# Scan of two directions: one group of transposes moved from round 5 of a step to round 3

## The chip, the cores and the metric

The kernel is one program on one core of a Trainium2 chip. The metric is the device time of one execution in microseconds (us). TensorE, VectorE, ScalarE and GpSimd each run their own queue in program order; semaphores order the queues against each other. SyncE issues the transfers.

## The reference, cut to what matters

Two blocks follow each other. The first has two layers; in each the tokens (16 meta tokens and 1024 others, L = 1040) pass through a latent attention and a bidirectional recurrence side by side, then through a mixture of experts. The recurrence has 8 heads with a 64 x 64 state each and runs once forward and once backward:

```python
def step(S, inp):
    r_t, w_t, k_t, v_t, kk_t, b_t = inp
    sa = jnp.einsum('bhvk,bhk->bhv', S, kk_t)
    S = S * w_t[:, :, None, :] - sa[..., None] * b_t[:, :, None, :] + v_t[..., None] * k_t[:, :, None, :]
    return S, jnp.einsum('bhvk,bhk->bhv', S, r_t)
```

Here b_t = kk * a. Two key forms enter the state: k (with its gate), "index 0", and -kk * a, "index 1". The change touches the second.

## The kernel before, in words

**The scan in chunks.** The scan doesn't go token by token. A step takes C = 104 tokens (two chunks of H = 52) of one direction; NT = 10 steps make one direction of a layer, so there are 2 layers x 2 directions x 10 = 40 steps. The tile `hb` holds the two key forms scaled by a running decay: index 0 from k (VectorE, L1570) and index 1 from kk * a (GpSimd L1638, then VectorE L1561). The tile `kr` holds the scaled kk and r (L1565, L1568). The products of hb and kr give the small matrices `Ab` (from index 1) and `Ak` (from index 0), which VectorE takes out of PSUM with a mask (L1576). From Ab comes a matrix `lm` (GpSimd masks, L1653), and from it T in five levels of products, `ps<-T,lm`, `ps<-XX,T`, `ps<-T,XX`. At the end of the step the state is advanced with the turned, that is transposed, hb: tile `m.tm`, named hbT in the profile, read only there.

**Rounds.** Each step is a list of phases in 23 rounds (`PHASES`): rounds 0 to 2 hold phases 0 to 10, round 3 phase 11, round 4 phase 12, round 5 phases 13 and 14, round 6 phase 15, rounds 7 to 22 phases 16 to 31. The backward direction runs 11 rounds (`STAGGER`) behind the forward one. In a round each engine does the phases of one direction, then a piece of an attention item (`att_pe`, `att_dve`), then the phases of the other direction; ScalarE does its longest attention piece, the exponentials, at the round's end. A direction in its rounds 0 to 3 comes second, else the forward one comes first. When one direction is in rounds 3 to 6, the other is in its last levels and then in its state products (`ps<-S,kr` and others).

**What the phases around the change do.**
- Phase 3: TensorE turns v (use 2); ScalarE copies it in phase 5.
- Phases 8 to 11: VectorE makes hb index 1, kr, and hb index 0. GpSimd makes rka in phase 11 (L1644).
- Phase 12: the first products, kr with hb index 1; phase 13: the second products, kr with hb index 0.
- Phase 14: TensorE turns hb index 0, then index 1, then multiplies for the bonus (`ps<-aa,rk`). ScalarE copies the three results. GpSimd makes lm with index 0.
- Phase 15: TensorE turns lm (`ps<-consts,lm`), VectorE adds the identity (L1581, L1585, L1588).

**Banks and uses.** A direction has two PSUM banks in the scan. The results of a step are numbered as uses; use n stands in bank n % 2, and before it is written `scan_free` waits until use n - 2 has been taken out, by ScalarE if its number is in `BY_ACT`, else by VectorE. Uses in the kernel before: 2 turned v; 3, 4 first products; 5, 6 second products; 7 turned hb index 0; 8 turned hb index 1; 9 bonus; 10 turned lm. A turn is written as a product with the identity, so in the trace turned hb is `ps<-consts,hb`, and each turn or product of the scan leaves two matmul records.

Of the kernel before, what the change touches and what calls it, by code (L numbers as in the profile page):

```python
# [1180 lines left out]
USES = 34  # L1181
LEVELS = 6
MASKS = {14: 0, 15: 1, 16: 2, 18: 3, 20: 4, 22: 5}
BY_ACT = {2, 7, 8, 9} | {13 + 3 * lv for lv in range(4)} | {25 + 4 * x + n for x in range(2) for n in (0, 1, 3)}
ODD = [(slice(64 * o, 64 * o + 64), slice(64 * o, 64 * o + H)) for o in range(2)]


# [63 lines left out]
def scan_bank(P, d, step, use):  # L1251
    return P.ps[2 * d + use % 2]
# [102 lines left out]
def scan_pe(e, P, li, d, step, ph):  # L1355
# [11 lines left out]
    if ph == 3:  # L1367
        scan_free(e, P, li, d, step, 2)
        b = scan_bank(P, d, step, 2)
        turns(e, P, [(b[r, 256 * ch + 64 * j:256 * ch + 64 * j + 64], rw.v[q, j, half(d, step, ch)])  # L1370
                   for ch in range(2) for j in range(4) for q, r in ODD]).then_inc(*pe.tick(*key, 2))
    if 12 <= ph < 14:
        e.wait_ge(*dv.at(*key, "kr1" if ph == 12 else "hb0"))
        mat = 1 if ph == 12 else 0
        for ch in range(2):
            use = 2 * ph - 21 + ch
            b, hs = scan_bank(P, d, step, use), slice(H * ch, H * ch + H)
            scan_free(e, P, li, d, step, use)
            at = [2 * H * (place(1, ch, j) // 4 * 2 + j // 2) for j in range(4)]
            mms(e, [(b[r, at[j]:at[j] + 2 * H].rearrange("p (a t) -> p a t", a=2),  # L1380
                     m.hb[q, mat, j, hs], m.kr[q, j, :, hs], True, True) for j in range(4) for q, r in ODD]
                ).then_inc(*pe.tick(*key, use))
    if ph == 14:
        for k in range(2):
            b = scan_bank(P, d, step, 7 + k)
            scan_free(e, P, li, d, step, 7 + k)
            turns(e, P, [(b[r, 256 * ch + 64 * j:256 * ch + 64 * j + 64], m.hb[q, k, j, H * ch:H * ch + H])
                       for ch in range(2) for j in range(4) for q, r in ODD]).then_inc(*pe.tick(*key, 7 + k))
        scan_free(e, P, li, d, step, 9)
        e.wait_ge(*po.at(*key, "rka"))  # L1390
        mms(e, [(scan_bank(P, d, step, 9)[32 * d:32 * d + 8, 0:C], rw.rk8[:, j, :], m.aa[:, j, :], j == 0, j == 3)
                for j in range(4)]).then_inc(*pe.tick(*key, 9))
# [43 lines left out]
    if ph >= 26:  # L1436
        x, part = divmod(ph - 26, 3)
        ch, S, use = m.chunks[x], m.S[x], 25 + 4 * x
        if part == 0:
            if x == 0:  # L1440
                e.wait_ge(*dv.at(*key, "T", 5))
                e.wait_ge(*ac.at(*key, "T", 5))
                e.wait_ge(*ac.at(*key, "ev", 2))
                e.wait_ge(*dv.at(*key, "ev", 6))
            else:
                e.wait_ge(*ac.at(*key, "ev", use - 1))
            e.wait_ge(*(dv.at(*key, "fS", x) if step or x else dv.at(li, d, "S0")))
            mms(e, state_rows(P, d, m, S, ch, m.vt[:, ch, :])).then_inc(*pe.tick(*key, use))
        if part == 1:
            e.wait_ge(*ac.at(*key, "ev", use))  # L1450
            mms(e, [(P.ps[2 * d + j % 2][r, 64 * (j // 2):64 * (j // 2) + 64], m.TT[c, 4 * ch + j, :],
                     m.rh[c, split_columns(j)], True, True) for j, o, r, c in quarters(range(4))]
                ).then_inc(*pe.tick(*key, use + 1))
        if part == 2:
            b = scan_bank(P, d, step, use + 2)
            mats = []
            for j in range(4):
                jc = slice(64 * j, 64 * j + 64)
                mats += [(b[q, jc], m.tm[r, 0, ch, jc], m.vt[r, ch, jc], True, False) for q, r in ODD]
                mats += [(b[q, jc], m.tm[r, 1, ch, jc], m.uu[r, split_columns(j)], False, True) for q, r in ODD]  # L1460
            e.wait_ge(*ac.at(*key, "ev", use + 1))
            mms(e, mats).then_inc(*pe.tick(*key, use + 2))
            mms(e, outputs(scan_bank(P, d, step, use + 3), m, S, ch, m.vt[:, ch, :])).then_inc(*pe.tick(*key, use + 3))


def scan_act(e, P, li, d, step, ph):
    rw, pe, dv, ac, po = P.rw, P.c("scan_pe"), P.c("scan_dve"), P.c("scan_act"), P.c("scan_pool")
    m, sl, key = P.scan[d], chunk(d, step), (li, d, step)

    def take(out, view, use):  # L1470
        e.wait_ge(*pe.at(*key, use))
        e.activation(out, view, ACT.Copy).then_inc(*ac.tick(*key, "ev", use))

    if ph == 1:
        e.wait_ge(*dv.at(*key, "ev", 0))
        e.activation(m.sig, m.sig, ACT.Tanh, scale=0.5).then_inc(*ac.tick(*key, "sig"))
        e.wait_ge(*dv.at(*key, "ev", 1))
        e.activation(m.aa, m.aa, ACT.Tanh, scale=0.5).then_inc(*ac.tick(*key, "aa"))
    if ph == 5:
        take(m.vt[0:HP].rearrange("p c n -> p (c n)"), scan_bank(P, d, step, 2)[0:HP, :], 2)  # L1480
    if ph == 5:
        e.wait_ge(*po.at(*key, "b"))
        for j in range(4):
            made = e.activation(m.aa[:, j, :], m.aa[:, j, :], ACT.Identity, bias=rw.par[:, 7, j:j + 1],
                                scale=rw.par[:, 1, j:j + 1])
        made.then_inc(*ac.tick(*key, "1+"))
    if ph == 6:
        e.wait_ge(*dv.at(*key, "x1"))
        e.activation(m.ei, m.cs if d == 0 else m.x1, ACT.Exp, scale=KAPPA).then_inc(*ac.tick(*key, "ei"))
    if ph == 7:  # L1490
        e.activation(m.eK, m.x1 if d == 0 else m.cs, ACT.Exp, scale=-KAPPA if d == 0 else KAPPA).then_inc(
            *ac.tick(*key, "eK"))
    if ph == 8:
        e.activation(m.ea, m.cs if d == 0 else m.x1, ACT.Exp, scale=-KAPPA).then_inc(*ac.tick(*key, "ea"))
    if ph == 9:
        e.wait_ge(*dv.at(*key, "f"))
        e.activation(m.f, m.f, ACT.Exp, scale=-0.5 * KAPPA).then_inc(*ac.tick(*key, "f"))
    if ph == 14:
        for k in range(2):
            take(m.tm[0:HP, k, :, :].rearrange("p c n -> p (c n)"), scan_bank(P, d, step, 7 + k)[0:HP, :], 7 + k)  # L1500
        take(rw.bon[d][:, sl], scan_bank(P, d, step, 9)[32 * d:32 * d + 8, 0:C], 9)
    if 16 <= ph < 26 and level_of(ph)[1]:
        lv = level_of(ph)[0]
        out, bank = joined(m.T)[0:HP, 1], joined_bank(P.ps[2 * d + 1])[0:HP]
        if lv < 5:
            take(out, bank, 10 + 3 * lv)
        else:
            e.wait_ge(*pe.at(*key, 24))
            e.activation(out[:, 1], bank[:, 1], ACT.Copy).then_inc(*ac.tick(*key, "T", 5))
    if ph >= 26:  # L1510
        x, part = divmod(ph - 26, 3)
        use = 25 + 4 * x
        if part == 0:
            take(halves(m.rh)[0:HP], P.banks[0:HP, 2 * d:2 * d + 2, 0:128], use)
        if part == 1:
            take(halves(m.uu)[0:HP], P.banks[0:HP, 2 * d:2 * d + 2, 0:128], use + 1)
        if part == 2:
            if step and x == 0:
                e.wait_ge(*P.d(f"scan_y{d}_out").at(li, step - 1, 3))
            take(m.ys[0:HP, m.chunks[x], :], scan_bank(P, d, step, use + 3)[0:HP, 0:256], use + 3)  # L1520


def scan_dve(e, P, li, d, step, ph):
# [47 lines left out]
    if 12 <= ph < 14:  # L1571
        dst = m.ab if ph == 12 else m.ak
        for ch in range(2):
            use = 2 * ph - 21 + ch
            e.wait_ge(*pe.at(*key, use))
            e.tensor_tensor(dst.rearrange("p (k c i) a t -> p k c i (a t)", k=2, c=2)[0:HP, :, ch],  # L1576
                            scan_bank(P, d, step, use)[0:HP, 0:416].rearrange("p (k i x) -> p k i x", k=2, i=2),
                            m.qmask, ALU.mult).then_inc(*dv.tick(*key, "ev", use))
# [51 lines left out]
def scan_pool(e, P, li, d, step, ph):  # L1630
# [14 lines left out]
    if ph in MASKS:  # L1645
        lv = MASKS[ph]
        if lv == 0:
            e.wait_ge(*dv.at(*key, "ev", 4))
        elif lv == 2:
            e.wait_ge(*dv.at(*key, "T", 0))  # L1650
        elif lv > 2:
            e.wait_ge(*pe.at(*key, 8 + 3 * (lv - 2)))
        e.tensor_tensor(m.LM[lv % 2][0:HP], m.ab[0:HP, :, 0, :],  # L1653
                        bc(m.lmask[0:HP, H * lv:H * lv + H].unsqueeze(1), [HP, 8, H]), ALU.mult).then_inc(
            *po.tick(*key, "lm", lv))
# [2721 lines left out]
```

## Time and profile before

| | |
|---|---|
| median of 3 runs | 5022.56 us (5014.44 to 5028.41) |
| profiled execution | 5016.12 us, its span 5014.2 us |
| mean granted TensorE clock | 0.955 |
| busy, share of the span | TensorE 90%, weight loads 76%, VectorE 64%, ScalarE 43%, GpSimd 24% |
| scan of layer 0 | 367 to 1135 us |
| scan of layer 1 | 2249 to 3020 us |

The busy shares are means over stages with different limits. In the scan the rounds of the two directions and the attention items are woven together, so the rows in order of time are the ones to read: "idle before" in brackets says how long the engine stood idle before the instruction and what ended it. Instructions of one kind that follow each other are merged into one row.

### The profile page before, as it was taken

To read this page: it belongs to the slowest core of one execution; us is meant where nothing else is said; L and a number is where in the kernel's file an instruction comes from. 1 tells how busy PE (TensorE), PEld (TensorE's weight loads), DVE (VectorE), ACT (ScalarE), POOL (GpSimd) and SP (SyncE) were. 2 spreads that over 40 slices of the span, in tenths; PEclk is the share of its full clock that TensorE was granted. 3 is DMA by queue.
4 is the path that set the end of the run, shared out by engine and by line. 5 is a ranking of instruction groups with operands and counts; after the bars stand their busy time and mean duration, and the time that the engine had idled before them with its cause. 6 is when DMAs were issued, how large, how long until landed. Compare 5 with 4: busy or idle time off the path is not lost. (4 is left out here: it accounts for less than half of the span.)

```text
span 5014.2 us, 126170 instructions
## 1 busy us (share of the span) xinstructions
PE 4497.6 (90%) x55574; PEld 3831.9 (76%) x55574; DVE 3209.2 (64%) x4913; ACT 2168.0 (43%) x3971; POOL 1220.1 (24%) x868
## 2 busy tenths in 40 slices
PE   6988888889799978988888889799979988999999
PEld 6887777776588857878778777688857647788887
DVE  5436666668788875346666569688874476561752
ACT  2433333333288863333333333388853252332431
POOL 0012222222244420002222222244421100222221
PEclk9999999999899988999999999899989889999999
DMA  5420111013366665420101013466751002333333
GB/s 145 149 59 19 36 22 33 21 42 112 120 241 251 256 200 136 126 57 21 35 20 34 20 47 126 171 243 259 263 202 46 22 1 101 106 93 126 111 107 97
DMA packets 379005, 535.80 MB, mean 107 GB/s; under 512 B 118165, under 2 KB 302549, under 8 KB 350413
## 3 DMA queue, kind: packets, MB, share of 16 engines
q1 hardware_dynamic: 335645, 488.54, 30.2%
q0 software_dynamic: 41472, 33.95, 2.2%
q8 instruction: 441, 7.23, 0.6%
q10 hardware_dynamic: 1344, 5.24, 0.3%
q14 instruction: 103, 0.84, 0.1%
HBM read 573.10 MB, written 121.92 MB: 139 GB/s over the span
## 5 line engine op out<-in xcount | busy, mean ns | idle before, releaser
L288 PE MATMUL ps<-w_hi,xbT 128*128 128x512 f32 x1536 | 502.9, 399 | 19.1 <-DVE w L2833 19.1
L288 PE MATMUL ps<-hT,w_in 128*128 128x416 f32 (+1 forms) x2736 | 491.5, 338 | 4.1 <-DVE hT L3113 4.1
L288 PEld LDWEIGHTS ps<-hT,w_in 128*128 128x128 f32 x2736 | 455.7, 194 | 29.6 <-issue 19.2
L2833 DVE TENSOR_TENSOR w<-w,w_hi 128x2048 fp32r<-128x2048 f32 x192 | 430.1, 2279 | 2.2 <-ACT w_hi L2790 2.2
L1653 POOL TENSOR_TENSOR lm<-Ab,consts 116x416 f32<-116x416 f32 x240 | 268.5, 1130 | 514.1 <-DVE T L1588 252.5
L2790 ACT ACTIVATE w_hi<-w 128x2048 fp32r<-128x2048 f32 x192 | 359.1, 1937 | 0.0
L288 PEld LDWEIGHTS ps<-w_hi,xbT 128*128 128x128 f32 x1536 | 290.9, 189 | 87.2 <-DVE w L2833 28.3
L288 PE MATMUL ps<-w,xbT 128*128 128x512 f32 x768 | 301.7, 393 | 0.0
L2864 DVE TENSOR_TENSOR w<-w,w_hi 128x2048 fp32r<-128x2048 f32 x96 | 223.3, 2326 | 97.2 <-ACT w_hi L2826 97.2
L288 PE MATMUL ps<-w_hi,actT 128*128 128x512 f32 x768 | 253.6, 391 | 4.9 <-DVE actT L2859 4.9
L288 PE MATMUL ps<-x1T,w_gate 128*128 128x512 f32 x1056 | 248.4, 391 | 3.0 <-DVE x1T L3800 1.6
L288 PE MATMUL ps<-x1T,w_up 128*128 128x512 f32 x1056 | 246.5, 389 | 0.0
L288 PE MATMUL ps<-w_down,act 128*128 128x512 f32 x1056 | 241.3, 391 | 3.1 <-POOL w_down L4026 3.1
L288 PEld LDWEIGHTS ps<-x1T,w_gate 128*128 128x128 f32 x1056 | 199.3, 189 | 45.2 <-issue 1.9
L288 PEld LDWEIGHTS ps<-w_down,act 128*128 128x128 f32 x1056 | 199.2, 189 | 44.8 <-POOL w_down L4026 3.5
L1596 DVE TENSOR_TENSOR XX<-ps,consts 116x416 f32<-116x416 f32 x200 | 117.7, 588 | 175.2 <-PE ps L288 174.7
L288 PEld LDWEIGHTS ps<-x1T,w_up 128*128 128x128 f32 x1056 | 198.3, 188 | 41.1
L4017 POOL TENSOR_TENSOR w_up<-w_up,w_up 128x1024 fp32r<-128x1024 f32 x44 | 116.4, 2646 | 458.1 <-ACT w_up L3939 458.1
L288 PE MATMUL ps<-w_out,mixT 128*104 128x512 f32 (+1 forms) x864 | 218.2, 406 | 10.5 <-DVE w_out L2171 5.8
L2779 POOL DMA_INDIRECT t_ys<-yo,slots x96 | 101.5, 1057 | 463.4 <-PE ps L295 384.7
L288 PEld LDWEIGHTS ps<-w_out,mixT 128*104 128x104 f32 (+1 forms) x864 | 151.7, 179 | 67.7 <-DVE w_out L2171 10.2
L794 POOL TENSOR_TENSOR w_in<-w_in,w_in 128x1024 fp32r<-128x1024 f32 x22 | 56.1, 2549 | 605.2 <-ACT w_in L809 605.2
(464 smaller groups left out, 11015.9 us busy)
## 6 DMA issues: line engine op xcount, KB each, us to landing
w<-in_moe_w_dram SPq DMA_DIRECT2D x192, 1024.0 KB, 12.5
w_gate<-in_w_gate_dram SPq DMA_DIRECT2D x44, 512.0 KB, 3.8
w_up<-in_w_up_dram SPq DMA_DIRECT2D x44, 512.0 KB, 3.9
w_down<-in_w_down_dram SPq DMA_DIRECT2D x44, 512.0 KB, 3.6
w_in<-in_w_in_dram SPq DMA_DIRECT2D x36, 512.0 KB, 4.9
w_out<-in_w_out_dram SPq DMA_DIRECT2D x24, 512.0 KB, 6.9
t_h<-x SPq DMA_DIRECT2D x20, 416.0 KB
kn<-t_kn SPq DMA_DIRECT2D x8, 1040.0 KB, 7.3
```

The source lines that it names most:

```text
L288: made = e.matmul(out, a, b, start=start, stop=stop)
L794: e.tensor_tensor(w.lo, w.x, w.hf, ALU.subtract).then_inc(*count.tick(li, "lo", n))
L1596: e.tensor_tensor(m.XX[0:HP].rearrange("p (k u) t -> p k u t", k=2), both_banks(P, d, 0)[0:HP].rearrange("p k (u t) -> p k u t", t=H), bc( ...
L1653: e.tensor_tensor(m.LM[lv % 2][0:HP], m.ab[0:HP, :, 0, :], bc(m.lmask[0:HP, H * lv:H * lv + H].unsqueeze(1), [HP, 8, H]), ALU.mult).then_i ...
L2779: e.indirect_dma_start(T["ys"], bass.IndirectOffsetOnAxis(P.slots[:, table_column(b - 2):table_column(b - 2) + 1], 0), m.yo[b % 2], None, ...
L2790: e.activation(w.hi, w.x, ACT.Copy).then_inc(*P.c("moe_act").tick(li, "w13", b, k))
L2833: e.tensor_tensor(w.lo, w.x, w.hf, ALU.subtract).then_inc(*P.c("moe_dve").tick(li, "w13", b, k))
L2864: e.tensor_tensor(w.lo, w.x, w.hf, ALU.subtract).then_inc(*dv.tick(li, "w2", b))
L4017: e.tensor_tensor(w.lo, w.x, w.hf, ALU.subtract).then_inc(*po.tick(0, c, "lo", f))
```

## The change

TensorE turns hb index 1 in phase 11 (round 3) and not in phase 14 (round 5); ScalarE's copy of it moves to phase 11 too. The turn is now use 3 and the uses after it are renumbered: 4, 5 first products; 6, 7 second products; 8 turned hb index 0; 9 and 10 as before. So the second of the first products (use 5) waits for ScalarE's copy of use 3, where it waited for ScalarE's copy of turned v; the turn of index 0 (use 8) waits for the first Ak to be taken, as before; the bonus (use 9) waits for the second Ak to be taken, where it waited for ScalarE's copy of turned hb. `BY_ACT` and the waits on "ev" numbers follow. No instruction that computes is added or taken away.

```diff
--- before.py
+++ after.py
@@ -1181,7 +1181,7 @@
 USES = 34
 LEVELS = 6
 MASKS = {14: 0, 15: 1, 16: 2, 18: 3, 20: 4, 22: 5}
-BY_ACT = {2, 7, 8, 9} | {13 + 3 * lv for lv in range(4)} | {25 + 4 * x + n for x in range(2) for n in (0, 1, 3)}
+BY_ACT = {2, 3, 8, 9} | {13 + 3 * lv for lv in range(4)} | {25 + 4 * x + n for x in range(2) for n in (0, 1, 3)}
 ODD = [(slice(64 * o, 64 * o + 64), slice(64 * o, 64 * o + H)) for o in range(2)]
 
 
@@ -1369,11 +1369,18 @@
         b = scan_bank(P, d, step, 2)
         turns(e, P, [(b[r, 256 * ch + 64 * j:256 * ch + 64 * j + 64], rw.v[q, j, half(d, step, ch)])
                    for ch in range(2) for j in range(4) for q, r in ODD]).then_inc(*pe.tick(*key, 2))
+    if ph in (11, 14):
+        k, use = (1, 3) if ph == 11 else (0, 8)
+        b = scan_bank(P, d, step, use)
+        scan_free(e, P, li, d, step, use)
+        e.wait_ge(*dv.at(*key, f"hb{k}"))
+        turns(e, P, [(b[r, 256 * ch + 64 * j:256 * ch + 64 * j + 64], m.hb[q, k, j, H * ch:H * ch + H])
+                   for ch in range(2) for j in range(4) for q, r in ODD]).then_inc(*pe.tick(*key, use))
     if 12 <= ph < 14:
         e.wait_ge(*dv.at(*key, "kr1" if ph == 12 else "hb0"))
         mat = 1 if ph == 12 else 0
         for ch in range(2):
-            use = 2 * ph - 21 + ch
+            use = 2 * ph - 20 + ch
             b, hs = scan_bank(P, d, step, use), slice(H * ch, H * ch + H)
             scan_free(e, P, li, d, step, use)
             at = [2 * H * (place(1, ch, j) // 4 * 2 + j // 2) for j in range(4)]
@@ -1381,11 +1388,6 @@
                      m.hb[q, mat, j, hs], m.kr[q, j, :, hs], True, True) for j in range(4) for q, r in ODD]
                 ).then_inc(*pe.tick(*key, use))
     if ph == 14:
-        for k in range(2):
-            b = scan_bank(P, d, step, 7 + k)
-            scan_free(e, P, li, d, step, 7 + k)
-            turns(e, P, [(b[r, 256 * ch + 64 * j:256 * ch + 64 * j + 64], m.hb[q, k, j, H * ch:H * ch + H])
-                       for ch in range(2) for j in range(4) for q, r in ODD]).then_inc(*pe.tick(*key, 7 + k))
         scan_free(e, P, li, d, step, 9)
         e.wait_ge(*po.at(*key, "rka"))
         mms(e, [(scan_bank(P, d, step, 9)[32 * d:32 * d + 8, 0:C], rw.rk8[:, j, :], m.aa[:, j, :], j == 0, j == 3)
@@ -1441,7 +1443,7 @@
                 e.wait_ge(*dv.at(*key, "T", 5))
                 e.wait_ge(*ac.at(*key, "T", 5))
                 e.wait_ge(*ac.at(*key, "ev", 2))
-                e.wait_ge(*dv.at(*key, "ev", 6))
+                e.wait_ge(*dv.at(*key, "ev", 7))
             else:
                 e.wait_ge(*ac.at(*key, "ev", use - 1))
             e.wait_ge(*(dv.at(*key, "fS", x) if step or x else dv.at(li, d, "S0")))
@@ -1495,9 +1497,10 @@
     if ph == 9:
         e.wait_ge(*dv.at(*key, "f"))
         e.activation(m.f, m.f, ACT.Exp, scale=-0.5 * KAPPA).then_inc(*ac.tick(*key, "f"))
+    if ph == 11:
+        take(m.tm[0:HP, 1, :, :].rearrange("p c n -> p (c n)"), scan_bank(P, d, step, 3)[0:HP, :], 3)
     if ph == 14:
-        for k in range(2):
-            take(m.tm[0:HP, k, :, :].rearrange("p c n -> p (c n)"), scan_bank(P, d, step, 7 + k)[0:HP, :], 7 + k)
+        take(m.tm[0:HP, 0, :, :].rearrange("p c n -> p (c n)"), scan_bank(P, d, step, 8)[0:HP, :], 8)
         take(rw.bon[d][:, sl], scan_bank(P, d, step, 9)[32 * d:32 * d + 8, 0:C], 9)
     if 16 <= ph < 26 and level_of(ph)[1]:
         lv = level_of(ph)[0]
@@ -1571,7 +1574,7 @@
     if 12 <= ph < 14:
         dst = m.ab if ph == 12 else m.ak
         for ch in range(2):
-            use = 2 * ph - 21 + ch
+            use = 2 * ph - 20 + ch
             e.wait_ge(*pe.at(*key, use))
             e.tensor_tensor(dst.rearrange("p (k c i) a t -> p k c i (a t)", k=2, c=2)[0:HP, :, ch],
                             scan_bank(P, d, step, use)[0:HP, 0:416].rearrange("p (k i x) -> p k i x", k=2, i=2),
@@ -1645,7 +1648,7 @@
     if ph in MASKS:
         lv = MASKS[ph]
         if lv == 0:
-            e.wait_ge(*dv.at(*key, "ev", 4))
+            e.wait_ge(*dv.at(*key, "ev", 5))
         elif lv == 2:
             e.wait_ge(*dv.at(*key, "T", 0))
         elif lv > 2:
```

## Rows read from the trace of the kernel before

**Rows 1.** Page, the chain that ended last, by engine, as share of the span.
```profile
PE 15%; DVE 1%; DMA 0%; issue 0%; SPq 0%; ACT 0%; POOL 0%; POOLq 0%; DVEq 0%
```

**Rows 2.** Stretches, both scans: from:to, length, busy us by engine, clock, DMA.
```profile
367.00:1135.00 768.00, 676.12 (x19597) 607.64 (x19597) 501.34 (x1090) 294.46 (x829) 211.27 (x197) 0.98 0.13 30
2249.00:3020.00 771.00, 670.51 (x19528) 610.75 (x19528) 472.99 (x1029) 278.85 (x765) 208.42 (x197) 0.95 0.14 35
```

**Rows 3.** Tile hb: its instructions, then what their engines waited for.
```profile
L288 PE MATMUL ps<-consts,hb x2560: 215/216/258, 372.2 to 2984.7; 64*52 64x64 f32 x197
...
  DVE kr L1568: 74.7, 40
```

**Rows 4.** TensorE in order of time, forward step: start, us, work, idle before.
```profile
669.61 1.54 PE L288 MATMUL ps<-kr,hb 64*52 64x104 f32 x30 [1.25 <-DVE kr L1568]
...
670.99 0.63 PE L288 MATMUL ps<-T,XX 52*52 52x52 f32 x30
673.19 1.63 PE L288 MATMUL ps<-kr,hb 64*52 64x104 f32 x32 [1.56 <-DVE Ab L1576]
674.79 2.00 PE L288 MATMUL ps<-consts,hb 64*52 64x64 f32 x64
676.72 0.88 PE L288 MATMUL ps<-aa,rk 128*8 128x104 f32 x8
```

**Rows 5.** VectorE in order of time, the same forward step.
```profile
668.46 0.58 DVE L1561 SCALAR_TENSOR_TENSOR hb<-hb,ei 128x416 f32<-128x416 f32 x1
668.97 0.58 DVE L1568 TENSOR_TENSOR kr<-u,ea 128x416 f32<-128x416 f32 x1
...
672.46 1.08 DVE L1576 TENSOR_TENSOR Ab<-ps,consts 116x416 f32<-116x416 f32 x2
...
674.15 1.30 DVE L1576 TENSOR_TENSOR Ak<-ps,consts 116x416 f32<-116x416 f32 x2 [0.32 <-PE ps L288]
...
678.19 1.09 DVE L1838 COPY pT<-ps 104x416 f32<-104x416 f32 x2 [2.48 <-PE ps L295]
```

**Rows 6.** ScalarE in order of time, the same forward step.
```profile
671.71 0.34 ACT L1509 ACTIVATE T<-ps 116x208 f32<-116x208 f32 x1 [2.86 <-PE ps L288]
...
673.58 0.20 ACT L1806 ACTIVATION_READ_ACCUMULATOR p<-ps,stat 104x1 f32 x1
675.94 0.60 ACT L1472 ACTIVATE hbT<-ps 116x512 f32<-116x512 f32 x1 [2.16 <-PE ps L288]
```

**Rows 7.** GpSimd in order of time, the same forward step.
```profile
672.62 1.07 POOL L1644 TENSOR_TENSOR aa<-u,aa 128x416 f32<-128x416 f32 x1 [4.84 <-DVE hb L1570]
```

**Rows 8.** TensorE in order of time, the backward step after it.
```profile
707.88 0.60 PE L288 MATMUL ps<-T,lm 52*52 52x52 f32 x31 [1.36 <-DVE T L1604]
...
714.44 1.99 PE L288 MATMUL ps<-consts,hb 64*52 64x64 f32 x64 [0.80 <-DVE Ak L1576]
716.36 0.88 PE L288 MATMUL ps<-aa,rk 128*8 128x104 f32 x8
```

**Rows 9.** VectorE in order of time, the same backward step.
```profile
706.15 0.58 DVE L1561 SCALAR_TENSOR_TENSOR hb<-hb,ei 128x416 f32<-128x416 f32 x1
...
721.16 0.59 DVE L1588 TENSOR_TENSOR T<-ps,consts 116x416 f32<-116x416 f32 x1 [4.98 <-PE ps L288]
```

**Rows 10.** Lines L1588 and L1838 on VectorE: idle before them, us, times.
```profile
  PE ps L288: 96.8, 22
...
  PE ps L295: 46.4, 20
```

**Rows 11.** A slow forward step: its stretch, then TensorE in order of time.
```profile
2549.00:2556.00 7.00, 6.14 (x104) 6.09 (x106) 5.64 (x15) 1.94 (x7) 3.12 (x3) 0.56 0.16 35
...
2549.86 2.84 PE L288 MATMUL ps<-kr,hb 64*52 64x104 f32 x30 [1.03 <-DVE kr L1568]
...
2552.66 0.90 PE L288 MATMUL ps<-T,XX 52*52 52x52 f32 x28
...
2555.76 2.00 PE L288 MATMUL ps<-consts,hb 64*52 64x64 f32 x64
```

## Prediction

> **What bounds the kernel now.** I read the chain that ended last first: followed back from the end, it covers only some 16% of the span, all of it long after the scan, so it can't price an edit in the scan [rows 1]. The view by stretches comes second. The two scans take 768 us (367 to 1135) and 771 us (2249 to 3020), 1539 us of 5014, with TensorE busy 88% and 87%, VectorE 65% and 61%, ScalarE 38% and 36% of the stretch [rows 2]. In this stage no engine is full; the order of each queue and the waits between queues set the time. So the change must be read round by round, and the reader should look at one thing: where TensorE stands idle around the old and the new place of the turns.
>
> The trace has 2560 matmuls of the turns, 64 for each of 2 layers x 2 directions x 10 steps = 40 steps; so one turn of an index (16 transposes in the code) is 32 of them. In the same view the wait for kr (L1568) stands before the products kr,hb 40 times, 74.7 us in all [rows 3]: weight load and matmul are counted each, so that is the 20 forward steps, some 37 us (the two first steps, which have no neighbour, have much of it).
>
> I then read one step of each direction in order of time.
>
> Forward (d = 0): hb with index 1 is made by VectorE at 668.46 to 669.04, kr at 668.97 to 669.55 [rows 5]. TensorE idles 1.25 us, then starts the first products at 669.61, the other direction's level at 670.99, idles 1.56 us for Ab, starts the second products at 673.19, the turns at 674.79 and the bonus at 676.72 [rows 4]. The attention's transposes follow it. From 673.19 on TensorE never stops until these are done. VectorE's pT copies at 678.19 had waited 2.48 us for these transposes [rows 5], ScalarE's copy of the first turn had waited 2.16 us [rows 6], and the T of L1588, which the rest of the step starts from, is queued on VectorE behind the pT copies. So in round 5 and 6 everybody waits for TensorE.
>
> Backward (d = 1): TensorE idles 1.36 us before T,lm at 707.88, hb with index 1 being ready at 706.73; later it idles 0.80 us for Ak, runs the turns from 714.44 and the bonus from 716.36 [rows 8, 9], and goes on without a stop to the turns of lm, for whose result VectorE's L1588 waits. VectorE stands idle for 4.98 us before L1588 [rows 9]. This is the rule over the run: pT copies (L1838) waited for TensorE 20 times, 46.4 us, and L1588 waited for it 22 times, 96.8 us [rows 10]. By the rows in order of time the 22 are the 20 backward steps and the first forward one of each layer, which has no attention beside it; the other 18 forward steps are among the 20.
>
> **The change part by part.**
>
> *Removed from round 5.* Both turns take 676.72 - 674.79 = 1.93 us, or 716.36 - 714.44 = 1.92 us; one takes 0.96 us [rows 4, 8]. Is the half that goes on the path? The turn that stays waits for the first Ak eviction as the first turn did (the use before the previous), so it starts where it did. The bonus product then needs three things. First, the second Ak eviction, which ends at 674.15 + 1.30 = 675.45, against a start at 674.79 + 0.96 = 675.75. Second, rka of GpSimd, ended at 672.62 + 1.07 = 673.69 [rows 7]. Third, the bank, which VectorE's eviction frees now and not ScalarE's copy. All three are early by 0.3 us or more, so the bonus and all behind it start 0.96 us earlier. The attention's transposes need the exponentials, whose last row ends at 673.58 + 0.20 = 673.78, long before even the bonus starts [rows 6]. The turns of lm need ScalarE's copy of the turn that stays, over at 675.94 + 0.60 = 676.54 [rows 6]; they stand behind the bonus, the transposes and the neighbour's products, so they come later. VectorE, ScalarE and GpSimd have only work behind TensorE then. I take the full 0.96 us as path in rounds 5 and 6.
>
> *Added to round 3.* Another direction's level and the attention stand ahead of the turn on TensorE, both as before. Latency from the end of kr to the products is 0.06 us (669.55 to 669.61) [rows 4, 5], so the forward turn starts at about 669.10 and ends at 670.06. The cover is the wait for kr up to 669.61; 0.45 us sticks out. The first products and the other direction's T,XX start that much later. Their users are far off: the first Ab eviction starts at 672.46 because VectorE comes to it only then, after the attention's maxima, while the products' last start is near 671.0; with 0.45 us more there is still a microsecond. TensorE's next idle time, 1.56 us before 673.19, takes up the rest [rows 4, 5]. So it costs nothing on the path. If that cover were gone it would cost 0.45 us a step.
>
> Backward, the turn runs from about 706.79 to 707.75, in the idle 1.36 us before T,lm at 707.88 [rows 8, 9]. Nothing sticks out.
>
> *ScalarE's copy* (0.60 us [rows 6]) moves with the turn. Its copy starts 675.94 - 674.79 = 1.15 us after the turn's start; forward this gives 670.25 to 670.85. Queued behind it on ScalarE are the neighbour's T (L1509), at 671.71, and the exponentials [rows 6]: not reached. The second of the first products now waits for this copy, a new wait: it would start at 670.9, where the first product (half of the 1.38 us of both, from 670.06) gives 670.75. Some 0.15 us more lateness, before the same spare time of VectorE. Behind this wait on TensorE stands T,XX only. The new numbers of the other banks name the same evictions of the same products in other words: lm with index 0 still waits for the second Ab. No transfer is moved.
>
> *Slow-clock steps.* Seven of the 20 forward steps have their rounds 3 and 4 at half the granted clock, by the view of stretches laid over each step. The nearest rows show such a step: 0.56 granted from 2549 to 2556, the lower level of 1.2 GHz for nearly all of it, and the products take 2552.66 - 2549.86 = 2.80 us against 670.99 - 669.61 = 1.38 us; TensorE runs on without a stop from 2549.86 to the turns at 2555.76 [rows 4, 11]. There the turn takes 0.96 x 2.80/1.38 = 1.95 us at most, of which about 0.5 us is covered: 1.45 us later, 0.96 us given back, 0.5 us lost. With the clock back up for the turn alone it would be 0.5 us gained. I take a loss of 0.2 us each.
>
> Sum: 33 x 0.96 = 31.7 us gained, 7 x 0.2 = 1.4 us lost, net 30 us. Bounds: 33 x 0.96 - 7 x 0.5 = 28 us, and 40 x 0.96 = 38 us if the clock stays up; if the forward cover fails as well, 20 x 0.45 = 9 us less, 19 us. The profiled execution took 5016.1 us and the median of the runs is 5022.6 (5014.4 to 5028.4). From the one I get 4986, from the other 4992; I write 4988.
>
> *A rule weighed.* The rows show the clock at the lower level just after TensorE's idle time of rounds 2 and 3 in those forward steps [rows 11], and the change puts work into this idle time. The Trainium skill, in TensorE: Matmul & The Clock Gate, What's actually happening, says that throttled is the default and activity releases it. By that rule some of the slow stretches would shorten; that is a rival below. This trace agrees as far as the slow stretches follow idle ones, but not every forward step with that idle time has one: the one at 669.61 runs at full speed.
>
> **The rivals.**
> (1) My forecast, 26 to 39 us gained: 0.68.
> (2) The clock rises: the seven slow steps become like the fast ones. From the first products to the turns a slow one takes 2555.76 - 2549.86 = 5.90 us, a fast one 674.79 - 669.61 = 5.18 us, 0.7 us less [rows 4, 11]. All 40 steps then gain 0.96 us and these seven 0.7 us more, 43 us together: 4973 to 4979. For it: the turn fills the idle time. Against: the granted clock differs between like steps already. 0.10.
> (3) Half is given back: something other than TensorE, such as Ak's second eviction with only 0.3 us to spare, or ScalarE, becomes last in rounds 5 and 6 and leaves 0.3 to 0.6 us a step. 12 to 25 us gained, 4994 to 5008. 0.12.
> (4) Hidden anyhow: the gain comes to stand in front of an idle time of TensorE later in the step (as is the 1.56 us before 673.19 [rows 4]) that a chain on another engine sets. Each such chain that I followed starts from a product, a turn or a T that is itself behind TensorE's queue of round 5 and 6, as L1588 is, so it moves too; this speaks against it. Time 5012 to 5022. 0.06.
> (5) Slower: the copy in round 3. TensorE's second product waits for ScalarE's copy, and ScalarE's copy for the turn. If ScalarE were held by other work ahead of the copy, Ab, lm and the second products would all slip. The spare time before the second Ab is about 1 us, so the copy must be late by over 1 us to cost anything, and by over 1 + 0.96 us to make a step slower. With a slip of 3 us in the 20 forward steps it would be 20 x (3 - 1.96) = 21 us slower less 19 us gained in the backward ones, about even; with both directions, 40 us slower, 5060. Against it: in round 3 the exponentials stand behind the copy in the queue, and ScalarE is idle for 2.86 us before L1509 [rows 6]. 0.04.
>
> **How the numbers follow.** A measurement of this kernel can tell about 0.3%, 15 us, from no change (the three runs span 14 us). (1), (2) and most of (3) are faster by more than that: 0.68 + 0.10 + 0.07 = 0.85. The rest of (3) and most of (4) are within it: 0.10. Slower: 0.05. The range from 4970 to 5008 takes in the likeliest case with the spread of the runs, the clock's rival, and most of (3).
>
> **What would show it.** Right: 32 turns before the kr,hb products, once a step; the wait for kr before kr,hb [rows 3] gone or nearly so, a shorter one for hb (L1561, about 0.7 us a forward step) in its place; ScalarE's hbT copies still 80, half of them in round 3; bonus about 0.96 us after the turns' start instead of 1.92; the waits in [rows 10] stay nearly as long less 0.96 us a time; both scan stages 14 to 19 us shorter, the rest unchanged. Wrong: VectorE waiting for the first Ab products, TensorE waiting for ScalarE's hbT before them, or a new wait for Ak at the bonus; then (3) or (5). If all moved as said but the scans were as long, (4).

## The result, and the profile after

| | kernel before | kernel changed |
|---|---|---|
| median | 5024.51 us (4 runs, 5014.44 to 5028.41) | 4980.14 us (4 runs, 4975.65 to 4985.30) |
| profiled execution | 5016.12 us | 4982.88 us |
| ratio | | 0.9922, 95% interval 0.9902 to 0.9942 |

The change made the kernel 0.8% faster: 39 us by the ratio, 44 us between the medians and 33 us between the two profiled executions. In these two the scans, from their first tanh (L1476 before) to their last state update (L1621 before), became 22 and 14 us shorter. The forecast was 4988 us, 4970 to 5008, from a sum of 30 us.

The forward step that answers to [rows 4], TensorE in order of time, changed kernel:

```profile
662.35 1.10 PE L288 MATMUL ps<-consts,hb 64*52 64x64 f32 x32 [0.84 <-DVE hb L1564]
663.25 1.71 PE L288 MATMUL ps<-kr,hb 64*52 64x104 f32 x30
...
664.81 0.63 PE L288 MATMUL ps<-T,XX 52*52 52x52 f32 x30
666.34 1.63 PE L288 MATMUL ps<-kr,hb 64*52 64x104 f32 x32 [0.89 <-DVE Ab L1579]
667.94 1.10 PE L288 MATMUL ps<-consts,hb 64*52 64x64 f32 x32
668.97 0.88 PE L288 MATMUL ps<-aa,rk 128*8 128x104 f32 x8
```

The turn of index 1 begins 0.15 us after VectorE has made it (662.20), and the first products begin 0.90 us later. Counted from the start of VectorE's hb row, that is 0.49 us later than in [rows 4, 5] (1.64 us against 1.15). The idle time before the second products shrank from 1.56 to 0.89 us. The second products begin as long after the end of hb as before: 666.34 - 662.20 = 4.14 us, and 673.19 - 669.04 = 4.15 us. The remaining turn keeps its place too (5.74 and 5.75 us), and the bonus begins 1.03 us after the turn's start, against 1.93.

VectorE in the same step, answering to [rows 5]:

```profile
661.61 0.59 DVE L1564 SCALAR_TENSOR_TENSOR hb<-hb,ei 128x416 f32<-128x416 f32 x1
...
665.61 1.08 DVE L1579 TENSOR_TENSOR Ab<-ps,consts 116x416 f32<-116x416 f32 x2
...
667.29 1.30 DVE L1579 TENSOR_TENSOR Ak<-ps,consts 116x416 f32<-116x416 f32 x2 [0.32 <-PE ps L288]
...
670.44 1.09 DVE L1841 COPY pT<-ps 104x416 f32<-104x416 f32 x2 [1.58 <-PE ps L295]
```

Ab and Ak stand where they stood after hb (4.00 and 5.68 us after the start of the hb row against 4.00 and 5.69), and the wait of the pT copies for TensorE is 0.90 us shorter than in [rows 5].

The backward step, TensorE, answering to [rows 8]:

```profile
698.36 1.10 PE L288 MATMUL ps<-consts,hb 64*52 64x64 f32 x32 [0.44 <-DVE hb L1564]
699.36 0.60 PE L288 MATMUL ps<-T,lm 52*52 52x52 f32 x31
...
705.92 1.10 PE L288 MATMUL ps<-consts,hb 64*52 64x64 f32 x32 [0.80 <-DVE Ak L1579]
706.95 0.88 PE L288 MATMUL ps<-aa,rk 128*8 128x104 f32 x8
```

Here 0.92 of the 1.36 us of idle time before T,lm is filled and 0.44 us are left. T,lm begins as long after hb as before (1.15 us), and the bonus again comes 1.03 us after the turn.

Over the run, what VectorE waited for before line L1591 (L1588 before), which answers to [rows 10]:

```profile
  PE ps L288: 78.6, 22
```

before line L1841 (L1838 before):

```profile
  PE ps L295: 30.4, 20
```

and what the engines waited for before instructions with the tile hb, which answers to [rows 3]:

```profile
  DVE hb L1564: 82.7, 80
...
  ACT hbT L1474: 2.2, 12
```

The first two lost 18.2 and 16.0 us. The wait for kr is gone and one for hb stands in its place, 80 times because matmul and weight load are counted each, now once in every step. The new wait for ScalarE's copy is there too: before a weight load in 12 of the forward steps, 0.19 us each, 2.2 us in all.

The steps are numbered 0 to 39 in order of time; even ones are forward. Measured from the start of its own hb row on VectorE, the time to the bonus fell by 0.89 to 0.90 us in 25 of 40 steps. The 15 others:

```
step           0     7    20    21    24    25    26    28    30    34    35    36    37    38    39
change, us  -0.06 -0.95 -0.77 -1.77 +0.57 -2.04 -0.53 -1.61 +0.21 -0.59 -2.04 -1.89 -0.55  0.00 -2.03
```

All 40 make -36.4 us. Five steps whose first products ran at half clock, that is at the lower granted level, in both traces (0, 20, 26, 30, 38) gained little or lost. Those that gained 1.6 us and more (21, 25, 28, 35, 36, 39) had their first products at half clock only before, step 28 all but 0.24 us of them. Steps 24 and 34 were slow only after. Step 7 was slow only before and gained no more than the fast ones; step 37 was at full clock in both, and why it gained less is open.

The backward step 25 shows one of these. Before, the stretch and then TensorE's row behind the idle time:

```profile
2436.00:2439.00 3.00, 3.00 (x63) 3.00 (x61) 2.35 (x5) 0.31 (x1) 1.04 (x2) 0.50 0.87 272
2434.91 0.60 PE L288 MATMUL ps<-T,lm 52*52 52x52 f32 x31 [1.75 <-DVE T L1604]
```

After, the same:

```profile
2406.70:2409.70 3.00, 2.72 (x85) 2.62 (x81) 2.67 (x6) 0.34 (x1) 1.64 (x2) 1.00 0.84 247
2404.63 1.10 PE L288 MATMUL ps<-consts,hb 64*52 64x64 f32 x32 [0.75 <-DVE hb L1564]
```

The granted clock was 0.50 before, behind 1.75 us of idle time, and 1.00 after, behind 0.75 us.

One of those that were slow in both (step 30, forward), the stretch and then TensorE, answering to [rows 11]:

```profile
2591.00:2598.00 7.00, 6.27 (x109) 6.10 (x110) 5.88 (x14) 1.36 (x4) 1.58 (x2) 0.51 0.15 35
```

```profile
2592.05 1.95 PE L288 MATMUL ps<-consts,hb 64*52 64x64 f32 x32 [0.73 <-DVE hb L1564]
2593.77 2.84 PE L288 MATMUL ps<-kr,hb 64*52 64x104 f32 x30
```

The turn takes 1.72 us at 1.2 GHz where it takes 0.90 at 2.4.

### The profile page after: what moved, and what is told of

It reads as the page before. It is cut to its first block and busy times, and to the rows that moved or that the text cites. A ratio compares the mean times of both kernels' runs of the same rounds, so it can differ in the third digit from the quotient of the medians.

```text
span 4980.8 us, 126250 instructions
## 1 busy us (share of the span) xinstructions
PE 4498.3 (90%) x55574; PEld 3827.1 (77%) x55574; DVE 3208.7 (64%) x4913; ACT 2167.2 (44%) x3971; POOL 1219.4 (24%) x868
```

## The experiments

Ratios are against the kernel before, run on the same chip in turn, with 95% intervals. "Half clock" is the time at the lower level, summed from the granted clock of the trace, from the first ACTIVATE of L1476 in a scan to its last state update (L1621; line numbers of the kernel before), both layers, one profiled execution each: 120 us in the kernel before, 98 us in the changed one. "At full clock" means the steps that had no half clock between hb and bonus in either of the two traces compared.

**No turn of index 1.**

```diff
-    if ph in (11, 14):
-        k, use = (1, 3) if ph == 11 else (0, 8)
+    if ph == 14:
+        k, use = 0, 8
...
-    mats += [(b[q, jc], m.tm[r, 1, ch, jc], m.uu[r, split_columns(j)], False, True) ...]
+    mats += [(b[q, jc], m.tm[r, 0, ch, jc], m.uu[r, split_columns(j)], False, True) ...]
```

> The changed kernel without the turn of hb index 1 and its copy at all (the state products read the turned index 0 in its place, so that part of the result is left out). It prices round 3. If the turn in round 3 is hidden, as forecast, this runs like the changed kernel, at most 5 us faster, by the steps with a slow clock. If the turn in round 3 costs its uncovered 0.45 us in each forward step, this is 9 us faster or more; if round 3 gives half back, 15 to 20 us faster than the changed kernel.

4986.20 us (6 runs), 0.9935 (0.9920 to 0.9951), half clock 146 us. It is not faster than the changed kernel (0.9922), and by the two intervals a net cost of 9 us or more in round 3 is excluded. The times don't separate the turn's cost from the clock, which was lower here; the traces do. At full clock the time from hb to the bonus is the same as in the changed kernel within 0.01 us in 21 of 22 steps. So the turn in round 3 costs nothing on this path.

**The turn also in round 3.**

```diff
+    if ph == 11:
+        b = scan_bank(P, d, step, 4)
+        scan_free(e, P, li, d, step, 4)
+        e.wait_ge(*dv.at(*key, "hb1"))
+        turns(e, P, [... m.hb[q, 1, j, H * ch:H * ch + H] ...]).then_inc(*pe.tick(*key, "early"))
```

> The kernel before, with a further turn of index 1 and a copy of it in round 3, in the other bank, and the old ones left in round 5. It adds what round 3 got and takes nothing from round 5. Hidden in round 3: within 5 us of the kernel before, 0 to 0.1% slower. A cost in round 3 of 0.45 us a forward step: 9 us slower. The rival in which ScalarE's copy in round 3 becomes the last wait: 20 us slower or more.

ScalarE copies the result at once, and the second half of the first products waits for this copy.

5018.14 us (12 runs), 0.9999 (0.9986 to 1.0012). Half clock was 80 us against 120 us, so the equal times alone could hide a cost that the clock paid back. They don't: at full clock the time from hb to the bonus is that of the kernel before within 0.01 us in 25 of 26 steps. The added turn is hidden, copy and wait included.

**Round 5 with its turn twice.**

```diff
+        for more in range(int(ph == 14)):
+            turns(e, P, [... m.hb[q, k, j, H * ch:H * ch + H] ...])
         turns(e, P, [... m.hb[q, k, j, H * ch:H * ch + H] ...]).then_inc(*pe.tick(*key, use))
```

> The changed kernel with the turn of index 0 in round 5 done twice over into the same bank, one copy after it. TensorE has 32 more records in round 5, ScalarE nothing more. If the gain is TensorE's time on the path of round 5, all of it comes back: like the kernel before, 34 to 40 us slower than the changed one. If it was ScalarE's second copy or the bank wait for it, this stays near the changed kernel (0 to 10 us slower).

5012.63 us (12 runs), 0.9993 (0.9981 to 1.0005), 36 us slower than the changed kernel by the ratios, where 34 to 40 us was expected. The gain is gone. TensorE in a forward step, and what VectorE waited for before L1594 (L1588 before):

```profile
677.67 2.00 PE L288 MATMUL ps<-consts,hb 64*52 64x64 f32 x64
679.60 0.88 PE L288 MATMUL ps<-aa,rk 128*8 128x104 f32 x8
```

```profile
  PE ps L288: 96.2, 22
```

Bonus 1.93 us after the turns and 96.2 us of waiting: both are the kernel before's [rows 4, 10], with ScalarE's copy and the bank wait left as in the changed kernel. At full clock all 27 steps take the time of the kernel before from hb to the bonus, within 0.01 us. So it was TensorE's time, not the copy.

**The bonus after the turns of lm.**

```diff
     if ph == 15:
...
         turns(e, P, [(b[r, u, :], m.LM[0][r, u, :]) for u in range(8) for q, r in ODD]).then_inc(*pe.tick(*key, 10))
+        scan_free(e, P, li, d, step, 9)
+        e.wait_ge(*po.at(*key, "rka"))
+        mms(e, [(scan_bank(P, d, step, 9)[32 * d:32 * d + 8, 0:C], rw.rk8[:, j, :], m.aa[:, j, :], j == 0, j == 3)
+                for j in range(4)]).then_inc(*pe.tick(*key, 9))
...
+    if ph == 15:
         take(rw.bon[d][:, sl], scan_bank(P, d, step, 9)[32 * d:32 * d + 8, 0:C], 9)
```

> The changed kernel with the bonus product (0.81 us on TensorE) and its copy after the turns of lm, in round 6, not before them in round 5. If rounds 5 and 6 are bound by TensorE's whole amount of work, nothing changes (within 5 us). If they are bound by what it does before L1588's input, the steps get up to 0.8 us shorter each, 10 to 32 us faster than the changed kernel.

4977.70 us (6 runs), 0.9914 (0.9899 to 0.9929). That is 4 us from the changed kernel and within the noise, as expected if TensorE's whole work binds rounds 5 and 6 and not its order. Between two hb rows, though, 22 steps without half clock were 0.14 us shorter on the mean, which the run below takes up.

**Two and three turns in round 3.** The loop as above with `int(ph == 11)` and `2 * int(ph == 11)`.

> The changed kernel with the turn in round 3 done twice over into the same bank, one copy after it. It measures how much cover round 3 still has. Forward, the first products start 0.96 us later still, at about 2.0 us after hb index 1, and their second half at about 2.9, against the second Ab eviction at 3.9: hidden. Backward it pushes T,lm by 0.85 us; in layer 0 VectorE comes to its result later anyway, in layer 1 it does not. Theory of cover: 0 to 10 us slower than the changed kernel. Rival, that TensorE's work in round 3 is on the path: 20 to 38 us slower.

> The same with three turns in round 3. Forward, the second half of the first products would start at about 3.8 us after hb index 1 and end at about 4.8, past the second Ab eviction at 3.9; backward T,lm is late by 1.8 us. Theory of cover: it is used up, 15 to 45 us slower than the changed kernel. If this is still free, the cover is larger than the rows of before said.

Twice: 4991.59 us (5 runs), 0.9950 (0.9931 to 0.9968). Thrice: 5018.61 us (10 runs), 1.0001 (0.9985 to 1.0016). The second turn costs 0.0028 to 0.0037 of the time, 14 to 19 us, more than the 0 to 10 expected: a miss. The third costs another 0.0051, 26 us, or 0.64 us a step for 0.96 us of work, within the expectation. The cover doesn't end at one point. At full clock the second turn left the time from hb to the bonus as it was within 0.01 us in 21 of 32 steps, and added 0.33 to 0.37 us in seven backward steps of the second scan, where the expectation had seen T,lm without cover. The third added 0.69 us or more in each of 11 forward steps, 0.1 us in eight of the backward ones and 0.5 us and more in the others. From hb to the bonus the second turn added 5 us over all 40 steps; the rest of its 14 to 19 us lies outside this stretch or in other executions and wasn't found.

**ScalarE's copy three and five times** (`range(2)`, `range(4)`).

```diff
+        for more in range(2):
+            e.activation(m.tm[0:HP, 1, :, :]..., scan_bank(P, d, step, 3)[0:HP, :],
+                         ACT.Copy).then_inc(*ac.tick(*key, "more", more))
+            e.wait_ge(*ac.at(*key, "more", more))
```

> The changed kernel with ScalarE's copy in round 3 made three times, one after the other, so that TensorE's second first-product gets its bank some 1.3 us later. Theory: forward this eats the spare time before the second Ab eviction (about 1 us), 0 to 10 us slower. The rival in which the copy is the critical wait of round 3: 1.3 us in each of 40 steps, 50 us slower.

> The same with the copy made five times, some 2.6 us later. Past the spare time of 1 us, so about 1.5 us in each forward step and some of the backward ones: 30 to 60 us slower than the changed kernel, that is about as slow as the kernel before or slower. It shows where the wait on the copy would have decided.

Three copies: 4998.15 us (5 runs), 0.9957 (0.9941 to 0.9972), 18 to 22 us slower than the changed kernel by the ratios, against 0 to 10 expected. Five: 5062.46 us (5 runs), 1.0079 (1.0060 to 1.0098), about 80 us slower against 30 to 60. Both sizes were missed, low. With three, at full clock, 0.17 us was added from hb to the bonus in nine of 11 forward steps, which fits a copy 1.24 us later and a spare time of about 1 us; but 0.46 us was added in seven backward steps of the second scan, which the expectation did not price. With five copies, TensorE and VectorE in a forward step:

```profile
689.54 1.10 PE L288 MATMUL ps<-consts,hb 64*52 64x64 f32 x32 [0.84 <-DVE hb L1569]
690.44 0.91 PE L288 MATMUL ps<-kr,hb 64*52 64x104 f32 x16
693.84 0.89 PE L288 MATMUL ps<-kr,hb 64*52 64x104 f32 x14 [2.49 <-ACT hbT L1474]
...
695.38 2.82 PE L288 MATMUL ps<-kr,hb 64*52 64x104 f32 x32
698.03 1.06 PE L288 MATMUL ps<-consts,hb 64*52 64x64 f32 x32
```

```profile
694.94 0.59 DVE L1584 TENSOR_TENSOR Ab<-ps,consts 116x416 f32<-116x416 f32 x1 [1.56 <-PE ps L288]
```

This is the slower rival at work: the second half of the first products waits 2.49 us for the copy, the second Ab 1.56 us for these products. And from the second products to the turn it is 2.65 us where it is 1.60 in the changed kernel: TensorE was granted 0.53 of its clock there, after the idle time. Over the run, before instructions with the tile hb:

```profile
  ACT hbT L1474: 180.3, 80
```

Matmul and weight load counted each, that is 90 us in 40 steps. Half clock rose to 180 us, and the mean granted clock of all five executions was 0.949, against 0.956 in the ten of the changed kernel. The expectation had counted only the wait beyond the spare time and nothing for the clock.

**Three runs on one chip.** The changed kernel, the one with the late bonus and the one without the turn once more.

> The changed kernel once more, on the chip of the two that follow, as their reference: 0.990 to 0.994 of the kernel before.

> The kernel with the bonus product after the turns of lm once more, now beside the changed kernel. The steps with full clock were 0.2 us shorter than in the changed kernel; over 40 steps that is 8 us, so 0.998 to 0.999 of it. If the 0.2 us was chance, 1.000.

> The kernel without the turn of index 1 once more, beside the changed kernel. The first time it was not faster, and its two scans had 146 us of half clock against 98 us. If the turn in round 3 keeps TensorE's clock up, it is again slower than the changed kernel by 3 to 12 us and again has more half clock. If that was chance, it is equal or up to 5 us faster.

Changed: 4974.02 us, 0.9913 (0.9895 to 0.9930), half clock 86 us. Late bonus: 4986.83 us, 0.9930 (0.9909 to 0.9951). No turn: 4989.86 us, 0.9943 (0.9924 to 0.9962), half clock 126 us (6 runs each). The changed kernel came out as expected. The late bonus is no gain: by the ratios it is 9 us slower than the changed kernel, with intervals that overlap. Of the two outcomes expected for it, 5 to 10 us faster or equal, that leaves the second. Between two hb rows the steps without half clock were shorter by only 0.07 us this time (24 steps), so the 0.2 us was chance or too small to tell. Its half clock was 99 us. The kernel without the turn is again the slower one, by 15 us where 3 to 12 was expected if the turn keeps the clock up. Its forward step, TensorE:

```profile
666.60 1.54 PE L288 MATMUL ps<-kr,hb 64*52 64x104 f32 x30 [1.25 <-DVE kr L1569]
...
670.18 1.63 PE L288 MATMUL ps<-kr,hb 64*52 64x104 f32 x32 [1.56 <-DVE Ab L1577]
671.78 1.10 PE L288 MATMUL ps<-consts,hb 64*52 64x64 f32 x32
```

Idle 1.25 and 1.56 us as in [rows 4], and the turn 5.18 us after the first products. The second scan of each, by stretch, first the changed kernel of this chip:

```profile
2225.00:2981.00 756.00, 658.71 (x19485) 598.30 (x19489) 477.40 (x1037) 282.54 (x774) 212.73 (x200) 0.97 0.14 35
```

```profile
2225.00:2981.00 756.00, 647.63 (x18673) 588.10 (x18671) 472.22 (x1026) 270.50 (x752) 212.56 (x200) 0.95 0.14 35
```

The granted clock is 0.97 with the turn and 0.95 without.

Where the difference arises can be read over all traces. In the three traces without a turn in round 3 (the kernel before, and the kernel without the turn twice) TensorE stands idle for 1.33 to 1.76 us in round 3 of every backward step, and in 17 of these 60 steps a stretch of half clock begins 1.3 to 2.7 us after the start of the hb row: 5 in the kernel before, 8 and 4 in the other two. With the turn there 0.31 to 0.75 us of idle time are left, and in the nine traces of such kernels (all but the one with five copies) none of the 180 backward steps has such a stretch. In the forward steps, where 0.84 us of idle time stays before the turn in the one shown, it is less clear. From 1.6 us before the hb row to 8 us after it, the two first steps left out, 5, 8 and 10 such stretches begin in the three traces without the turn, and 4 to 7 in each of the nine with it.

## Why the prediction was right

**Removed from round 5: right, and the size nearly.** One turn was on the path of all 40 steps. The prediction named 0.96 us, half of both turns. Measured are 0.90 us: from the first turn to the bonus it was 1.93 us with two turns and is 1.03 us with one, so the second had added less than half. From one hb row to the next, in the 20 steps without half clock in either trace, the step shortened by 1.02 us on the mean and 0.95 on the median, with a scatter that comes mostly from idle times of TensorE that no other engine ended ("issue"). With the turn doubled in round 5 the whole gain is lost.

**Added to round 3: right.** 0.45 us was to stick out forward and did so (0.49), under VectorE's late Ab; backward nothing. The runs without the turn and with it in both places put its cost from hb to the bonus at 0.00 us a step at full clock.

**ScalarE's copy: right.** No more than 0.15 us of lateness forward was forecast; the rows have 12 waits of 0.19 us. The slower rival is real as a mechanism, with 2.6 us of further delay it made the kernel slower than before, but at one copy it is far from its point. The spare time of about 1 us holds forward (1.24 us more cost 0.17 us); what the prediction had no price for is the backward steps of the second scan, where the same delay cost 0.46 us, and the clock.

**Slow-clock steps: the term that was mis-sized.** The sum had 31.7 us from 33 steps and a loss of 1.4 us in seven. To the bonus, the 33 gave 31.8 us, but by luck: 0.90 us each and not 0.96, four backward steps (21, 25, 35, 39) that gained 1.8 to 2.0 us since they had half clock only before, and three (24, 34, 37) that gained 2.1 us less than the 0.90 each. The prediction had looked for slow steps among the forward ones alone; five backward ones had half clock behind their idle time too. The seven (0, 20, 26, 28, 30, 36, 38) gained 4.7 us where a loss was forecast. Five of them stayed slow and gained 0.2 us each on the mean, one reason being that the turn takes 1.72 us at the lower level and not 1.95; two (28, 36) were not slow any more, or hardly. That is the 6 us between the sum and the 36.4 us found.

**The rivals.** (4), hidden anyhow, and (3), half given back, fell with the first run. (2), the rising clock, was given 0.10, and the time alone doesn't tell it from (1): it had 4973 to 4979, and the changed kernel took 4980 and, run again, 4974. The traces do. The seven slow forward steps did not all become fast, as (2) had it; five stayed slow. But its mechanism acts in the backward steps, where the prediction had not looked: the stretches of half clock behind the idle time of round 3 are gone in the nine traces named above. In the pair of traces that is worth about 4 us of the 36.4 (steps 7, 21, 25, 35, 39, beyond 0.90 us each), and the two steps that were slow only after (24, 34) took 1.8 us of it back. That agrees with the rule of the Trainium skill weighed ahead (TensorE: Matmul & The Clock Gate, What's actually happening), that activity releases the throttle. This trace bears it out in the backward steps, while among the forward ones about as many were slow after (6 begin near the hb row) as before (5). Without the turn the scans had 146 and 126 us of half clock, with it 98 and 86, and on the shared chip the kernel without the turn took 0.9943 (0.9924 to 0.9962) against 0.9913 (0.9895 to 0.9930). That kernel carries other numbers in its state, but the kernel before carries the true ones and has the same stretches.

It isn't the chance of one execution either. The mean granted clock over the whole program was 0.953 in the 49 executions of the kernel before on the three chips of the experiments, 0.952 in the 12 without the turn, 0.956 in the 10 of the changed kernel and 0.957 in the 12 with the turn in both places. Other things move it as well, for with the late bonus it was 0.954 in 12. The execution profiled before had 0.955, more than the mean of its kernel; that may be why the two traces differ by 33 us and the medians by more. What the clock is worth in the medians is not shown.

The stretch read ahead ends the first scan at 1135 us, but its last state update is some 30 us later, and in the second scan some 15 us later. No term of the sum hangs on it.

## What to carry to other kernels

Where two queues of dependent work are woven together, price a moved group twice: by the engine's unbroken run at the old place (who waits there for this engine alone?) and by the idle time at the new place, up to the first consumer that is late for another reason. Cover runs out by degrees and not in all steps at once: the first turn in round 3 was free, the next cost about 0.4 us a step on the mean, the third 0.64. Look through the steps of both directions and both layers, not one of each: here the backward steps of the second layer lost their cover first. A new wait with slack is harmless until its source is late, so its slack belongs in the price.

## What the runs showed of the hardware

The idle time that a wait makes can be followed by a lower clock, and that has to be priced with it. Behind 1.33 to 1.76 us of idle time in round 3 of the backward steps, half clock followed in 17 of 60 steps; behind 0.31 to 0.75 us at the same place, in none of 180. Three such steps (25, 35, 39) were 1.14 us longer for it. With five copies the wait was 2.49 us in the forward step shown, and 1.05 us more went to the products after it, which ran for most of that time at 1.2 GHz (granted clock 0.53; 2.65 us to the turn against 1.60). Put the other way, taking 0.90 us of work out of TensorE's queue in round 3 did not make the kernel faster in either of two comparisons: 0.9935 and 0.9943 against 0.9922 and 0.9913.
